# Moving TensorE's activation buffers in SBUF: the bytes between them and the weights, modulo 256

## The reference, cut to what matters

```python
def swiglu(x, w_gate, w_up, w_down):
    return (jax.nn.silu(x @ w_gate) * (x @ w_up)) @ w_down
...
x = x + 0.5 * swiglu(rms_norm(x, norm_ffn1[l]), ffn1_w_gate[l], ffn1_w_up[l], ffn1_w_down[l])
x = x + hybrid_mixer(rms_norm(x, norm_mix[l]), w_in[l], ...)
x = x + 0.5 * swiglu(rms_norm(x, norm_ffn2[l]), ...)
...
up = jnp.einsum("bsnc,ncd->bsnd", branches, w_branch[l])
gates = jax.nn.sigmoid((h @ w_gate[l]).reshape(bsz, seq, N_BRANCH, D_MODEL))
mix = jnp.einsum("bsnd,bsnd->bsd", gates, up) @ w_o[l]
...
f = (jax.nn.gelu(gate, approximate=True) * val) @ ffn_w_down[l]
```

## Time and profile before

| | |
|---|---|
| median of 3 runs | 2256.14 us |
| the profiled execution | 2260.43 us, its span 2258.6 us |
| TensorE busy with matmuls | 2194.0 us, 97% |
| weight loads busy | 2116.4 us, 94% |
| VectorE busy | 1498.1 us, 66% |
| ScalarE busy | 1099.0 us, 49% |
| GpSimd busy | 126.4 us, 6% |
| granted TensorE clock, mean | 0.983 |
| DMA | 163 GB/s mean |

### The profile page before, as it was taken

How to read it: one execution, slowest core, us unless ns; L and a number is a source line. 1 busy time by engine, 2 the same in 40 slices (tenths; PEclk the granted TensorE clock), 3 DMA queues, 4 the chain that set the end, 5 groups by cost and what they waited for, 6 DMA issues and landing times.

```text
span 2258.6 us, 40842 instructions
## 1 busy us (share of the span) xinstructions
PE 2194.0 (97%) x17948; PEld 2116.4 (94%) x17952; DVE 1498.1 (66%) x1812; ACT 1099.0 (49%) x1334; POOL 126.4 (6%) x118
## 2 busy tenths in 40 slices
PE   8999999999999999999999899999999899999998
PEld 8999999999999999999998798989989889899998
DVE  5556757555655775755568986667756898666775
ACT  5435465444534445544443656555544256654553
POOL 0001000000100100100000000010000000001000
PEclk9999999999999999999999899999989999998999
DMA  7555435555555543465653443545544344353552
GB/s 253 191 184 168 164 125 167 198 187 187 180 187 179 184 150 113 168 205 190 204 158 118 145 146 117 172 134 192 187 147 150 114 150 131 113 187 112 188 187 75
DMA packets 285044, 367.26 MB, mean 163 GB/s; under 512 B 10002, under 2 KB 257730, under 8 KB 284610
## 3 DMA queue, kind: packets, MB, share of 16 engines
q1 hardware_dynamic: 281138, 361.01, 48.2%
q10 hardware_dynamic: 3728, 3.62, 0.5%
HBM read 363.56 MB, written 1.05 MB: 161 GB/s over the span
## 4 chain that ended last, share of the span: by engine, by line
PE 85%; DVE 9%; ACT 4%; issue 1%; DMA 1%; POOL 0%; ACTq 0%; SPq 0%; POOLq 0%; DVEq 0%
PE ps L624 25%; PE ps L625 24%; PE ps L626 24%; DVE wlo L1802 3%; ACT whi L1289 2%; PE ps L668 1%; PE ps L707 1%; PE ps L709 1%; PE ps L708 1%; DVE sq L2410 1%; PE ps L1056 1%; PE ps L1073 1%; PE ps L1083 1%; PE ps L1104 1%; DVE arena L2089 0%
## 5 line engine op out<-in xcount | busy, mean ns | idle before, releaser
L624 PE MATMUL ps<-hhi,whi 128*128 128x256 f32 x3808 | 1085.9, 285 | 14.8 <-DVE wlo L1802 5.8
L626 PE MATMUL ps<-hhi,wlo 128*128 128x256 f32 x3808 | 1074.7, 282 | 0.0
L625 PE MATMUL ps<-hlo,whi 128*128 128x256 f32 x3808 | 1067.6, 280 | 0.0
L1802 DVE TENSOR_TENSOR wlo<-raw,whi 128x2048 fp32r<-128x2048 f32 (+1 forms) x347 | 782.0, 2255 | 428.2 <-ACT whi L1289 428.1
L1289 ACT ACTIVATE whi<-raw 128x2048 fp32r<-128x2048 f32 (+1 forms) x347 | 652.3, 1882 | 732.2 <-PE ps L626 642.7
L624 PEld LDWEIGHTS ps<-hhi,whi 128*128 128x128 f32 x3808 | 722.4, 190 | 32.1 <-issue 12.9
L625 PEld LDWEIGHTS ps<-hlo,whi 128*128 128x128 f32 x3808 | 715.5, 188 | 4.9 <-issue 4.3
L626 PEld LDWEIGHTS ps<-hhi,wlo 128*128 128x128 f32 x3808 | 712.6, 187 | 0.3
L624 PE MATMUL ps<-hidhi,whi 128*128 128x256 f32 x1056 | 298.0, 282 | 1.0 <-DVE hidlo L2170 1.0
L625 PE MATMUL ps<-hidlo,whi 128*128 128x256 f32 x1056 | 298.4, 283 | 0.0
L626 PE MATMUL ps<-hidhi,wlo 128*128 128x256 f32 x1056 | 296.4, 281 | 0.0
(11 more groups left out here) (284 smaller groups left out, 2111.4 us busy)
## 6 DMA issues: line engine op xcount, KB each, us to landing
raw<-in_ffn_w_up SPq DMA_DIRECT2D x88, 1024.0 KB, 5.1
raw<-in_w_in SPq DMA_DIRECT2D x68, 1024.0 KB, 5.1
raw<-in_ffn_w_down SPq DMA_DIRECT2D x66, 1024.0 KB, 4.8
raw<-in_ffn_w_gate SPq DMA_DIRECT2D x43, 1024.0 KB, 5.1
raw<-in_w_gate SPq DMA_DIRECT2D x32, 1024.0 KB, 5.3
raw<-in_w_branch SPq DMA_DIRECT2D x16, 1024.0 KB, 4.9
raw<-in_nsa_cmp_w SPq DMA_DIRECT2D x8, 1024.0 KB, 5.5
raw<-in_w_out SPq DMA_DIRECT2D x6, 1024.0 KB, 4.8
```

The costliest lines, as they stand in the source:

```text
L624: pe.matmul(o, w_hi, m_hi, start=start, stop=False, skip_group_check=True)
L625: pe.matmul(o, w_hi, m_lo, start=False, stop=False, skip_group_check=True)
L626: return pe.matmul(o, w_lo, m_hi, start=False, stop=stop, skip_group_check=True)
L1802: dve.tensor_tensor(wlo[:, slot, 0:n], raw[:, slot, 0:n], whi[:, slot, 0:n].bitcast(F32), ALU.subtract) \
```

## The change

Only the unused tensors between the buffers change: four of them, of 128, 32, 192 and 32 bytes, in place of six of 64. The two halves of a pair now have the same start modulo 256: `hhi` and `hlo` 128, `hidhi` and `hidlo` 160, `brhi` and `brlo` 96. The sum is 384 bytes as before, so `xT` and all that follows keep their addresses. No instruction is added, removed, moved or resized; only addresses of these six buffers in them differ.

```diff
-        def phase(n):
-
-            return sb(f"phase{n}", 16)
-
-        phase(0)
+        def phase(n, cols):
+
+            return sb(f"phase{n}", cols)
+
+        phase(0, 32)
         hhi = view(sb("hhi", KC * SEQ, F32R), c=KC, t=SEQ)
-        phase(1)
         hlo = view(sb("hlo", KC * SEQ, F32R), c=KC, t=SEQ)
-        phase(2)
+        phase(1, 8)
         hidhi = view(sb("hidhi", 2 * 2 * SEQ, F32R), b=2, c=2, t=SEQ)
-        phase(3)
         hidlo = view(sb("hidlo", 2 * 2 * SEQ, F32R), b=2, c=2, t=SEQ)
-        phase(4)
+        phase(2, 48)
         brhi = view(sb("brhi", 2 * BRC * SEQ, F32R), b=2, c=BRC, t=SEQ)
-        phase(5)
         brlo = view(sb("brlo", 2 * BRC * SEQ, F32R), b=2, c=BRC, t=SEQ)
+        phase(3, 8)
         xT = view(sb("xT", KC * SEQ), c=KC, t=SEQ)
```

## The result

The changed kernel takes 2266.96 us (median of 9 runs) against 2256.14 us (median of 9): ratio 1.0045, interval 1.0031 to 1.0058. It is slower by 10.8 us (by the interval 7 to 13), where I forecast 24 us less.

The account below looks back on a forecast made before the run. TensorE's own pace was taken as the bound. Savings of 20.1 + 4.8 + 0.4 + 0.6 = 25.9 us, times 0.92 = 23.8, took 2260.43 to 2236.6, times 0.9981 gave 2232 us; eight-in-ten range 2195 to 2272.

Parts of the forecast that it names:

- The bound: Whole kernel: TensorE's own pace from matmul start to start sets the time; its suppliers are not late.
- 0.92: Share of the saving in TensorE's steps let through to the end time: 25.9 us became 23.8 us.
- What a start modulo 256 costs: Step after a matmul by operand distance: worst at 0 (120 ns), then 64 (119), 192 (117 or more), best 128 (115 to 117).
- the normed input: 3792 trios of matmuls on hhi/hlo, all at distance 128: steps of 116 ns, 5.3 ns saved a trio, 20.1 us.
- At 160: Feed-forward rows, 1056 trios: step of 116.3 ns taken between neighbours 128 and 192, 4.8 us saved.
- at 96: Branch rows, 320 trios: step of 117.3 ns taken between 64 and 128, 0.4 us saved.
- A: Rival for the trios' pace: a conserved total, starts only hand delay between steps; 2256 us, chance 0.13.
- B: Rival: equal starts are bad, all steps become 120 ns, 32 us slower, 2288 us; chance 0.25, mostly in weaker form.
- C: Rival: interference vanishes at the best distance, all steps fall to 113 ns, 65 us saved, 2191 us; chance 0.10.
- The last sentence of the prediction: Forecast is wrong if the step depends on the order of starts between matmuls, not on the distance between the operands.
- The rule of the two ports: Skill's rule for TensorE's reads, priced as a rival: no start could matter, the time would stay at 2256 us.

Follow-up runs that it names:

- e3: Buffer starts changed from the kernel before: normed input 0/0, feed-forward rows 64/64, branch rows 32/32; 2275.05 us, ratio 1.0087.
- e10: Unequal halves against the kernel before: normed input 128/192, feed-forward rows 192/128, branch rows 0/192; 2277.67 us, ratio 1.0104.
- e11: Starts off a multiple of 32 against the kernel before: normed input 200/200, feed-forward rows 184/184, branch rows 248/248; 2282.32 us, ratio 1.0124.
- e4: Buffer starts changed from the kernel before: normed input 192/192, feed-forward rows 96/96, branch rows 224/224; 2240.29 us, ratio 0.9934.
- e9: All six buffers at start 192, against the kernel before; 2225.42 us, ratio 0.9866.
- e15: The same program as e9 run again, all six buffers at 192; 2227.55 us, ratio 0.9862 against the kernel before.
- e13: All six buffers at 192 plus 24 small foreign matmuls heading the first four column blocks of each feed-forward; 2216.64 us, ratio 0.9818 against the kernel before.
- e2: Buffer starts changed from the kernel before: normed input 160/160, feed-forward rows 128/128, branch rows 192/192; 2260.96 us, ratio 1.0023.
- e7: e4 with its six buffers and the weights all moved up by 64 bytes; 2242.60 us, ratio 0.9953 against the kernel before.
- e8: Normed input 256/256, feed-forward rows 320/320, branch rows 352/352, against the kernel before; one run of 2274.54 us.

## Why the prediction was wrong

**The bound: right.** TensorE's step is the pace, its suppliers stay ahead (5.4 us of waits), and 0.92 of the steps' change reached the end: 10.7 us worked out, 10.8 measured. The factor holds for the larger losses too. Worked out from the traces with 0.92, and measured in the same executions at equal clock, e3 is 22 and 22 us slower, e10 25 and 25, e11 32 and 31. The kernels with gains at 192 fall short of it by 2 to 6 us: e4 is 19 and 15 us faster, e9 31 and 28, e15 37 and 31, e13 with its kicks counted 46 and 44. What takes these few microseconds stays open. In medians the gains look smaller still (38 us for e13), since the faster kernels happened to be granted a little less clock.

**The step that failed** is "What a start modulo 256 costs": I put each single step down to the distance of the matmul that it follows. From 115 ns after the one matmul at 128 I took 116 for three of them, which made the 20.1 us of the normed input; measured, that term is a loss of 11 us. The rows showed a repeating pattern of 118, 115, 120 whose parts belong together; the 115 was the easy part of a cycle, and the 120 stood right behind it. The changed kernel shows it outright: one distance, five different steps, mean 118.8. What I should have trusted was the mean of a trio alone, and of that there were two values, equal, and from unequal halves: no basis for a curve. My interpolations failed too. At 160 (116.3, measured 117.3) the sign held, at 96 (117.3, measured 120.0) it did not: between 64 (117.8) and 128 (118.8) the curve rises to 120.0.

**What held of it.** With equal halves the mean step goes by the distance between the two operands modulo 256 (e2, e4, e7, e8), and this holds for both roles with the sign turned (token products). It is not quite all: at 160 the column block has 117.8 and the down product 117.4, a difference that no run explains.

**The rivals.** A, a conserved trio, was nearest in time for the changed kernel (2256, measured 2267) and is wrong as a cause: the trio goes from 340 to 360. B had the direction right. Its steps of 120 each are what happens at distance 0 (e3: 120, 120, 120), but equal starts are not bad as such: at 192 they are the best of all. C, the interference vanishes at the best distance, I gave 0.10 at 128; it is real, at 192, where a stretch either has it wholly or not at all. The last sentence of the prediction named what would make it wrong: that the order of starts counts rather than the distance. Half of that was so. The mean of equal halves goes by the distance; single steps, and the mean of unequal halves (e10), depend on the neighbours.

**The rule of the two ports.** The Trainium skill ("SBUF — State Buffer", "Who interferes with whom") has two independent read ports and a TensorE that never waits. Rows say otherwise of the step: places of the buffers alone move it from 113.3 to 120.1 ns and the time from 2225 to 2282 us. The Trainium skill's 109 ns for 256 columns ("TensorE: Matmul & The Clock Gate", "Back-to-back issue gap"), which that section gives without the weight load, was reached in no stretch of these; 113.3 was the least that repeated. That the moving operand and the weight load get in each other's way is the reading that fits the distance as the variable; no run here has such a matmul without its load, so this cause is argued and not shown. It would also have to say why the 128-column products, with the same loads, don't feel it. What carries a regime on at 192, and what draws it at a break, no run shows either.

## What to carry to other kernels

When the same matmul shape shows different steps from start to start, measure the mean over whole cycles and never the single step: neighbouring steps belong together. Try the starts of moving operands against the weights modulo 256 bytes in steps of 32, equal for all operands that take turns, and don't expect the places between two good ones to be good. It costs only padding and was worth 1.4% here. At the best place look for two regimes, since 24 small foreign matmuls were worth another 0.5%; use few, for each cost 0.14 us. Compare traces by steps rather than by spans: two executions with the same span hid 10 us. If whole times must be compared, compare runs of the same mean granted clock.

## What the runs showed of the hardware that I had not expected

- The step of a 256-column float32r matmul with its 128-column weight load depends on the distance between the operands modulo 256, from 113.3 to 120.1 ns, sharply: 113.3 or 118 at 192, 119.9 at 184, 120.1 at 200. The same product with 128 columns does not (111.6 to 111.7 in all traces).
- At 192 two regimes exist and last for as long as matmuls follow without a break, 1440 here. They are drawn at a break, differently in two executions of one program, and a foreign matmul that costs 0.14 us tips nearly all stretches to the fast one.
- The cycle of the steps need not be that of the loop: five matmuls at 128 and at 160, six at 96, in a loop of three.
- In this kernel 0.001 of mean granted clock is worth 1.5 us, over 72 runs.
